# Turning eight sample rows on chip, a new order of two additions, and a norm moved up, in a hybrid RWKV-7 / sparse-attention step with 32 experts

## The reference, cut to what matters

```python
def step(s, z):
    r_t, w_t, k_t, v_t, a_t, b_t = z
    sa = jnp.einsum('bhij,bhj->bhi', s, a_t)
    s = s * w_t[:, :, None, :] + sa[..., None] * b_t[:, :, None, :] + v_t[..., None] * k_t[:, :, None, :]
    return s, jnp.einsum('bhij,bhj->bhi', s, r_t)
...
y = ((y - mu) * lax.rsqrt(var + A_GN_EPS)).reshape(b, t, A_WIDTH) * ln_x_w.astype(f32) + ln_x_b.astype(f32)
y = y + (jnp.sum(r * k * r_k.astype(f32), axis=-1, keepdims=True) * v).reshape(b, t, A_WIDTH)
```

## Time and profile before

| | us |
|---|---|
| median of 3 runs | 1398.83 (1396.55 to 1401.09) |
| profiled execution: span from the first to the last instruction | 1409.7 |
| profiled execution: the time of its own run | not given with the profile |
| PE busy in the span | 1342.0 (95%) |
| DVE / ACT / POOL busy | 502.2 / 203.1 / 82.1 |
| expert stage, from about 480 us on | some 930 of the 1409.7 |
| mean granted TensorE clock | 0.989 |

### The profile page before, as it was taken

One profiled execution on the slowest core, in us unless ns is written; L12 is line 12 of the kernel. 1 busy time (PEld: TensorE's weight loads), 2 busy tenths in 40 slices (PEclk: granted clock), 3 DMA queues, 4 the chain that ended last, 5 costly groups with the idle time before them and its releaser, 6 DMA issues.

```text
span 1409.7 us, 21167 instructions
## 1 busy us (share of the span) xinstructions
PE 1342.0 (95%) x8689; PEld 660.6 (47%) x8690; DVE 502.2 (36%) x1090; ACT 203.1 (14%) x425; POOL 82.1 (6%) x109
## 2 busy tenths in 40 slices
PE   8998889899999999999999999999999999999996
PEld 6887776677778533333333333333333333333332
DVE  4455547444451523233222422242223322233223
ACT  3221122323310300001000100010000100001002
POOL 3002023230000000000000000000000000000000
PEclk9999999999999999999999999999999999999998
DMA  7345329275579599999999999999999999999994
GB/s 217 120 125 181 64 88 267 64 259 179 176 232 380 222 423 430 430 429 430 431 431 431 431 431 431 431 431 431 431 431 431 431 431 431 431 431 431 431 430 168
DMA packets 86308, 476.01 MB, mean 338 GB/s; under 512 B 12706, under 2 KB 53140, under 8 KB 61352
## 3 DMA queue, kind: packets, MB, share of 16 engines
q1 hardware_dynamic: 79256, 452.26, 79.1%
q0 software_dynamic: 5552, 21.77, 4.3%
q10 hardware_dynamic: 1440, 1.11, 0.2%
HBM read 471.66 MB, written 8.56 MB: 341 GB/s over the span
## 4 chain that ended last, share of the span: by engine, by line
PE 40%; DMA 25%; DVE 1%; ACT 0%; issue 0%; SPq 0%; DVEq 0%; ACTq 0%
DMA ring<-in_w_up 25%; PE bank L2602 22%; PE bank L2613 9%; PE bank L2542 3%; PE bank L2576 2%; PE bank L2550 1%; PE bank L2530 1%; PE bank L2524 1%; PE bank L2557 0%; PE bank L2129 0%; DVE ring L2475 0%; PE bank L2122 0%; ACT ring L2360 0%; DVE ex_work L2409 0%; DVE ex_work L2412 0%
## 5 line engine op out<-in xcount | busy, mean ns | idle before, releaser
L2602 PE MATMUL bank<-ring,ex_work 128*64 128x512 f32 x2032 | 448.7, 595 | 11.9 <-DMA ring<-in_w_up 11.9
L2602 PEld LDWEIGHTS bank<-ring,ex_work 128*64 128x64 f32 x2032 | 140.8, 137 | 311.7 <-issue 281.1
L2613 PE MATMUL bank<-ring,ex_work 128*64 128x512 f32 x1024 | 231.7, 596 | 0.0
L2405 DVE TENSOR_SCALAR ex_work<-bank 128x512 f32<-128x512 f32 x32 | 22.1, 692 | 426.9 <-PE bank L2602 426.9
L2613 PEld LDWEIGHTS bank<-ring,ex_work 128*64 128x64 f32 x1024 | 70.0, 136 | 138.4 <-issue 126.8
L2394 DVE TENSOR_TENSOR x<-bank,x 128x512 f32<-128x512 f32 (+1 forms) x192 | 117.1, 669 | 29.9 <-PE bank L2542 29.9
L2542 PE MATMUL bank<-ex_work,ex_back 64*128 64x512 f32 x384 | 91.1, 606 | 1.5 <-ACT ex_work L2319 1.5
L2313 ACT ACTIVATE ex_work<-ex_work 128x512 f32<-128x512 f32 x32 | 20.2, 632 | 432.8 <-DVE ex_work L2405 432.8
L616 PE MATMUL bank<-hT,w_group 128*128 128x264 f32 (+1 forms) x336 | 75.8, 386 | 0.0
L616 PEld LDWEIGHTS bank<-hT,w_group 128*128 128x128 f32 (+1 forms) x336 | 62.2, 186 | 12.6 <-issue 0.7
L1430 PE MATMUL bank<-hT,w_cmp 128*128 128x264 f32 x256 | 64.3, 398 | 2.9 <-PEq L990 1.3
(11 more groups left out here) (514 smaller groups left out, 1294.2 us busy)
## 6 DMA issues: line engine op xcount, KB each, us to landing
ring<-in_w_up SPq DMA_DIRECT2D x127, 2048.0 KB, 21.2
ring<-in_w_down SPq DMA_DIRECT2D x64, 2048.0 KB, 29.3
w_group<-in_w_in SPq DMA_DIRECT2D x12, 1024.0 KB, 5.3
w_cmp<-in_w_in SPq DMA_DIRECT2D x8, 1024.0 KB, 8.5
ring<-in_w_out SPq DMA_DIRECT2D x8, 512.0 KB, 7.1
out_win_s<-in_state_win_kv POOLq DMA_DIRECT2D x1, 4088.0 KB, 23.1
x<-in_x_prompt SPq DMA_DIRECT2D x4, 512.0 KB, 5.4
win_rows<-in_state_win_kv SPq DMA_DIRECT2D x4, 512.0 KB, 5.4
```

Source lines behind the costliest of these rows:

```text
L2405: nc.vector.tensor_scalar(g[:], banks[0][:], 7.0, None, ALU.min).then_inc(S["g_ready"], 1)
L2602: mm = mmul(banks[n // 2][lo:lo + SLOTS, :], B["xT"][:, k % 4, SLOTS * (k // 4):SLOTS * (k // 4) + SLOTS], (ninth[:, k, :] if e_ninth and ...
L2613: mm = mmul(banks[4][SLOTS * n:SLOTS * n + SLOTS, :], B["hT"][:, k % 4, SLOTS * (k // 4):SLOTS * (k // 4) + SLOTS], slot_of(8 + 4 * half + ...
```

## The change

Three parts. (1) In `rwkv_chunks` DVE adds to Y first and to X second, with a semaphore for each (`y_ready`, `x_ready`); `t1` waits for Y alone and `dxy` for X. The second pair of bonus sums moves on PE from level 2 to level 3, and its products on DVE from i = 6 to i = 7. (2) The samples' `ysm` is no longer stored and loaded: PE turns it whole, 128 partitions to 32, in job 8, and DVE puts it into y with four copies of 32 partitions; job 8 leaves ACT. (3) Job 8 moves from half step 23 to 18 and jobs 9 to 16 from 24 to 31 to 19 to 22 and 25 to 28; the squares and `normalised` move one round up with them.

```diff
-                        if i < N - 2:
-                            dve.wait_ge(x_ok.sem, 2)
-                            step(tt_(X[:, bs], X[:, bs], blocks(2 + i % 2), ALU.add))
-                        tt_(Y[:, bs], Y[:, bs], blocks(4 + i % 2), ALU.add).then_inc(xyr, 1)
+                        tt_(Y[:, bs], Y[:, bs], blocks(4 + i % 2), ALU.add).then_inc(yr, 1)
+                        if i < N - 2:
+                            dve.wait_ge(x_ok.sem, 2)
+                            tt_(X[:, bs], X[:, bs], blocks(2 + i % 2), ALU.add).then_inc(xr, 1)
...
-                        if i in (4, 6):
-                            for m in (i - 4, i - 3):
+                        if i in (4, 7):
+                            for m in ((0, 1) if i == 4 else (2, 3)):
...
                         if i >= 2:
-                            pe.wait_ge(xyr, i - 1)
+                            pe.wait_ge(yr, i - 1)
                             pe.wait_ge(t1e, i - 1)
...
                             pe.wait_ge(rb_ok.sem, 2)
+                        else:
+                            pe.wait_ge(xr, i - 1)
...
                         dxy(2 * l)
-                        if l in (1, 2):
+                        if l == 1:
                             pe.wait_ge(ake, 2)
-                            bonus_sums(2 * (l - 1))
+                            bonus_sums(0)
+                        if l == 3:
+                            bonus_sums(2)
                         dxy(2 * l + 1)
...
-                at_half = [3, 4, 6, 8, 10, 12, 14, 16, 23, 24, 25, 26, 27, 28, 29, 30, 31]
-                on_act = (3, 4, 5, 6, 7, 8, 13, 14, 15, 16)
+                at_half = [3, 4, 6, 8, 10, 12, 14, 16, 18, 19, 20, 21, 22, 25, 26, 27, 28]
+                on_act = (3, 4, 5, 6, 7, 13, 14, 15, 16)
...
-                    sp.wait_ge(y_parts.sem, 2)
-                    for i in range(2):
-                        sp.dma_start(heads(scratch["rwkv_out"])[:, half * i:half * i + half], ysm[n_h * i:n_h * i + n_h, :]).then_inc(s_stored, 16)
-                    sp.wait_ge(s_stored, 32)
-                    sp.dma_start(ys, scratch["rwkv_out"]).then_inc(sy_in, 16)
                     sp.wait_ge(hid, 64)
                     for g in range(2):
                         gate_weights(sp, g)
-                    sp.wait_ge(sy_in, 16)
...
-                        for m in ((0, 1) if b == 12 else (2, 3) if b == 13 else ()):
-                            act.wait_ge(set_d, 4 + m)
+                        for m in ((0, 1) if b == 11 else (2, 3) if b == 12 else ()):
+                            act.wait_ge(set_d, 5 + m)
...
+                            elif i == 8:
+                                by_head = banks[3][0:half, 0:P].rearrange("p (w b m j) -> p w j m b", w=2, b=TS, m=4)
+                                for w_half in range(2):
+                                    for j in range(2):
+                                        lo = HD * j + half * w_half
+                                        ins = nc.vector.tensor_copy(y[lo:lo + half, :, TP:T], by_head[:, w_half, j])
+                                ins.then_inc(set_d, 1)
...
-                        for m in {14: (0,), 15: (1, 2)}.get(b, ()):
+                        for m in {13: (0,), 14: (1, 2)}.get(b, ()):
                             normalised(m)
...
                         elif i == 8:
-                            pe.wait_ge(sy_in, 16)
-                            for m in range(4):
-                                mm = nc.tensor.transpose(banks[3][:, TS * m:TS * m + TS], ys[:, P * m:P * m + P], ident[0:TS, 0:TS])
+                            pe.wait_ge(y_parts.sem, 2)
+                            mm = nc.tensor.transpose(banks[3][0:half, 0:P], ysm[:], ident)
```

More of the change, by code:

```diff
@@ L699, in rwkv_chunks @@
                 l_ok, y_ok, x_ok, rb_ok, ak_ok, rk_ok = (Signal("m_%s_ready" % z) for z in ("L", "Y", "X", "RB", "AK", "RK"))
-                lmr, t1d, t1e, dxd, xyr = sem("level_ready"), sem("t1_done"), sem("t1_ready"), sem("dxy_done"), sem("xy_ready")
+                lmr, t1d, t1e, dxd, yr, xr = sem("level_ready"), sem("t1_done"), sem("t1_ready"), sem("dxy_done"), sem("y_ready"), sem("x_ready")
                 akd, ake = sem("av_done"), sem("av_ready")
@@ L918, in _ @@
                     for tt in range(2):
-                        pe.wait_ge(xyr, N - 1 + tt)
+                        pe.wait_ge(yr, N - 1 + tt)
                         for b, g, gs in both_parts:
@@ L998, in compress @@
                 e = spare[:, NF:NF + 4 * T].rearrange("p (m t) -> p m t", m=4)
-                ys = spare[0:TS, NF + 4 * T:NF + 4 * T + 512]
                 sS, vec, val, sa, ysm, s_in, wkv_out = (C[z] for z in ("sS", "vec", "val", "sa", "ysm", "s_in", "wkv_out"))
@@ L1003, in compress @@
                 bonus, y = (pT[:, 4 * i:4 * i + 4, :] for i in range(2))
-                s_parts, y_parts, s_stored, sy_in = Signal("sample_state_done"), Signal("sample_summed"), sem("sample_stored2"), sem("sample_y_in")
+                s_parts, y_parts = Signal("sample_state_done"), Signal("sample_summed")
                 eps = sb(st, "gn_eps", [P, 1])
@@ L1042, in _ @@
                     sp.dma_start(B1[:], bass.AP(b, P, [[1, P], [NX, 8], [1, TP]])).then_inc(bin_, 16)
-                    heads = lambda t: t.rearrange("b (h d) -> (b h) d", h=8)
                     sp.wait_ge(s_parts.sem, 2)
@@ L1088, in _ @@
                                 nc.scalar.activation(qg[:, i - 3, :], banks[3][:, 0:T], ACT.Copy, scale=SCALE).then_inc(set_a, 1)
-                            elif i == 8:
-                                copy(y[:, :, TP:T], banks[3][:, 0:4 * TS].rearrange("p (m t) -> p m t", m=4)).then_inc(set_a, 1)
                             elif i >= 13:
@@ L2732 @@
 CONST_NAMES = ("c_masks", "c_carry", "c_hot", "c_cmp_seen", "c_cols", "c_samples", "c_numbers", "c_rank", "c_dest", "c_pick")
-SCRATCH = [("rwkv_in", (6, TS, 512), F32), ("rwkv_out", (TS, 512), F32),
-           ("bias", (8, NX), F32), ("h", (T, D), F32)]
+SCRATCH = [("rwkv_in", (6, TS, 512), F32), ("bias", (8, NX), F32), ("h", (T, D), F32)]
 INS = ['x_prompt', 'x_sample', 'cache_cmp_kv', 'cache_sel_kv', 'state_win_kv', 'state_rwkv', 'state_rwkv_shift', 'page_table',
```

## The result

The changed kernel took 1390.42 us (median of 4 runs, 1390.21 to 1394.42) beside 1399.96 us for the kernel before (4 runs, 1396.55 to 1402.71): ratio 0.9935 with a 95% interval of 0.9915 to 0.9954, 9.1 us less. Run again on another occasion it took 1389.11 beside 1400.68 us, ratio 0.9923 (0.9905 to 0.9940), 10.8 us less. The forecast was 1386.5 us and a gain of 12.3 us, with a range of 1382.5 to 1392.5 us: the direction and the place of most of the gain were right, the size was some 1.5 to 3 us too large.

The account below looks back on a forecast made before the run. The experts' weight stream was taken to set the end, its start hanging on PE's work in front. 4.2 us (chunk levels) plus 8.1 (compress) made 12.3 off the median 1398.8: 1386.5 us, range 1382.5 to 1392.5.

Parts of the forecast that it names:

- The gain carries to the end: Expert stage: every microsecond won in front moves the weights' stream and the end by one microsecond.
- rivals 2 and 4: 2: ring absorbs front's gain, 1398.8 us, chance 0.03; 4: late copies in compress drop the clock, 1405.8 us, chance 0.02.
- Chunk levels, 4.2 us (2.6 to 4.9): `rwkv_chunks`: 0.7 us at `t1(3)` plus 3.5 us from `dxy(4)` to `t1(9)`, 4.2 us less.
- the pause of 0.87 us: PE's pause at `t1(5)`, no releaser: may swallow its 0.7 us gain; a second like it lowers the bound to 2.6.
- Compress, 8.1 us: `compress`: 7.7 us from round 9 to the last `layer1` plus 0.4 us in the tail; bounds 6.5 and 8.4.
- the removed wait ahead of job 8: `compress`: PE's wait of 4.47 us for the samples' rows to be reloaded goes.
- No wait takes the place of the removed one: `compress`, job 8: its input is there at 234.3, the turns ahead end at 237.15, 2.8 us to spare.
- The four DVE copies: `compress`, round 9: putting the turned rows into y costs 0.7 to 1.6 us, taken as 0.8, beside `layer1`.
- The copy for position 31: `compress`, DVE behind two `normalised`: ends near 7.3 us after round 14 starts, wanted near 7.7, 0.4 us left.
- Rival 1: Another stretch of 5 us falls to half clock, 2.5 us of work lost: 1389.0 us, chance 0.10.
- Rival 3: `compress`, rounds 13 to 15: POOL operations hold DVE copies, 2.6 us of idle PE: 1389.1 us, chance 0.10.
- Rival 5: The change doesn't do what it says, jobs still wait; with only the chunk part working 1394.6 us; chance 0.03.

Follow-up runs that it names:

- compress_only: Kernel before with parts (2) and (3), chunk levels as before: 1394.90 us, ratio 0.9954 (0.9937 to 0.9972).
- before_w1_late: Kernel before with the load of the first half of `w_cmp` put behind `t1(9)`, not paced: 1402.88 us, ratio 1.0011 (0.9998 to 1.0024).

## Why the prediction was right, and where its sizes were off

**The gain carries to the end: right.** Expert stage 911.0 to 912.1 us in all traces; rivals 2 and 4 fall.

**Chunk levels, 4.2 us (2.6 to 4.9): too large.** This is the step that failed. Alone it timed 0.6 us (-1.1 to 2.4); in traces the stage is 1.6 to 2.3 us shorter, like compared with like. The layout of the levels was right, with one size off: all the named waits vanished, and the new one is 0.50, not 1.0. With the load out of the way the levels won 5.0 us, and from `dxy(4)` to `t1(9)` they took some 12.3 us (154.92 to 167.2), forecast 12.45. But the working took the pause of 0.87 us in the earlier trace rows as an event that might at worst swallow 0.7 us of one wait and come once more. It is a cost that can come at any border of 253 instructions while the weights land. Under the old levels' waits it was mostly covered: of the three traces with the old levels and the paced load only the first has pauses in them. With the waits gone it stands bare, 2.5 to 3.3 us in two pauses in each of the six traces with the new levels and the paced load. In three of these six the clock then fell behind the second pause. The row was read; its cause wasn't asked for.

**Compress, 8.1 us: the mechanism right, the size too large.** 75.3 to 68.0 us in the second profiles and to 68.1 in `compress_only` are 7.2 us; the forecast's bounds were 6.5 to 8.4. The kernel alone timed 6.4 (3.9 to 8.8). All traces together agree with the timing more than with the sum: the six with the old block have 72.8 to 75.7 us, 74.5 in the mean, the five with the whole new one and its weights issued as in the changed kernel 67.2 to 70.4, 68.3 in the mean, so 6.2 us. The term that was sized too large is the removed wait ahead of job 8: 4.47 us in the forecast's trace is the longest of six (the others 2.83 to 3.99), and behind the shortest the clock stayed at 1.00. On the other side a new wait can come. The first profile of the changed kernel won only 4.9 against 75.3 by the same reading, since the wait of 3.89 us came and the clock fell behind it. "No wait takes the place of the removed one" looked at job 8 alone, not at the next transfer that PE needs. That wait appears when PE gets to it sooner than the weights. It was 0.63 us in the second profile of before, 1.93 in `before_w1_late`, so it comes without the change too; the longest, 3.38 and 3.89 us, were seen with the change only.

**The small terms.** The four DVE copies took 0.76 us together, forecast 0.8. The copy for position 31 ended at 258.49 at the latest (257.80 + 0.69), its prompt's part at 258.79, and the last `layer1` isn't interrupted. The bias copies follow 0.85 us of idle DVE.

**Rival 1**, the clock falling elsewhere, holds in part: 0.83 from 230 to 240 us in one profile. The 0.78 in the first 15 us of compress in the other is no new place, since the second profile of before has 0.77 there. **Rival 3**, POOL holding DVE: the copy of line 1149 took 0.40 us beside the POOL operation of 258.02, as in the earlier trace rows, and nothing waited for it. **Rival 5** falls: both parts do what they say.

**The total.** 2.3 + 7.2 = 9.5 us by the second profiles, timed 9.1 (6.4 to 11.9) and 10.8 (8.4 to 13.3), forecast 12.3. The smaller of the two is the forecast's own lower bound of 9.1; the time fell inside the stated range because the runs' scatter had been added to the bounds. The parts don't add up well: 0.6 and 6.4 us alone are 7.0 where both together timed 10.8 on the same occasion. The intervals allow it, but that the gains add, as the forecast has it, is not shown by the times. That the medians of 1392 to 1394 us go with the wait for the weights' second half is only argued: the profiled run with the wait took 1394.42, but one without it 1392.01.

## What to carry to other kernels

A short pause with no releaser in a row of small products is worth a look at the instruction queue's packets: one ends every few microseconds anyway, so look whether pauses of several traces follow the packets at one distance and are a whole block of instructions apart, and move the load beside them. If they go with it, taking out waits elsewhere will uncover them. When a wait on a transfer goes, ask which transfer the engine needs next, and how early that can land at the DMA load of the stage. Profile the kernel before twice ahead of subtracting: its first trace here was 8 us longer than its second.

## What the hardware showed that I had not expected

- Blocks of instructions seem to come late behind data. With 2 MB of weights issued in 5.7 us, no instruction packet started for 8.6 us and PE stood 4.80 us.
- A slower PE can cost nothing: with the granted clock at 0.78 over the first 15 us of compress PE came 3.2 us later to the second half's weights, and the block was 2.4 us shorter, since the wait of 3.89 us and the clock of 0.83 behind it didn't come. The other traces with the on-chip turn and both halves' loads go the same way: at a clock of 1.00 over these 15 us PE waited 3.89 and 3.38 us for the weights, at 0.89 2.02, 1.36 and 0.63 us, at 0.78 not at all, twice.
